# Expert gate and up projections in groups of 1024 columns, over two PSUM banks each

## The reference, cut to what matters

```python
def swiglu(h, w_gate, w_up, w_down):
    return (jax.nn.silu(h @ w_gate) * (h @ w_up)) @ w_down
...
for e in range(N_EXPERTS):
    y = y + combine[..., e:e + 1] * swiglu(h, w_gate[e], w_up[e], w_down[e])
```

## Time and profile before

| | |
|---|---|
| median of 3 runs | 1862.31 us (1860.47 to 1862.36) |
| the profiled execution | 1858.9 us, of which the span of its instructions is 1857.2 us |
| PE busy | 1701.4 us, 92% of the span |
| DVE busy | 1293.8 us, 70% |
| ACT busy | 1052.4 us, 57% |
| moved by DMA | 491.7 MB, 265 GB/s over the span |
| span of the items' loop | 825.2 to 1835.6 us |
| from one item's `YE` to the next one's | 126.1 to 126.2 us, twice about 124.4 us |

### The profile page before, as it was taken

One profiled execution on the slowest core, in us unless ns is written; L12 is line 12 of the kernel. 1 busy time (PEld: TensorE's weight loads), 2 busy tenths in 40 slices (PEclk: granted clock), 3 DMA queues, 4 the chain that ended last, 5 costly groups with the idle time before them and its releaser, 6 DMA issues.

```text
span 1857.2 us, 24273 instructions
## 1 busy us (share of the span) xinstructions
PE 1701.4 (92%) x9295; PEld 1464.4 (79%) x9295; DVE 1293.8 (70%) x1092; ACT 1052.4 (57%) x915; POOL 72.8 (4%) x94
## 2 busy tenths in 40 slices
PE   4986989998999887939999999999999999999995
PEld 4964989998999777928878878778788787787884
DVE  3796255545954256348878878888788788787885
ACT  3534244434342156237777777677777776777772
POOL 2014000000000100010000000000000000000001
PEclk9998799999987799969999999999999999999997
DMA  6525059656566223639999999999999999999992
GB/s 237 179 68 161 21 176 336 224 171 197 167 197 226 85 71 104 229 126 349 380 318 396 359 329 387 341 356 374 320 390 364 320 393 356 349 378 329 377 369 82
DMA packets 236653, 491.70 MB, mean 265 GB/s; under 512 B 8665, under 2 KB 66137, under 8 KB 236328
## 3 DMA queue, kind: packets, MB, share of 16 engines
q1 hardware_dynamic: 227088, 456.60, 68.6%
q0 software_dynamic: 9504, 34.24, 5.5%
HBM read 463.87 MB, written 27.42 MB: 265 GB/s over the span
## 4 chain that ended last, share of the span: by engine, by line
issue 57%; PE 31%; DVE 8%; ACT 2%; DMA 1%; POOL 1%; POOLq 0%; SPq 0%; ACTq 0%; DVEq 0%
PE bank L613 7%; PE bank L614 7%; PE bank L615 7%; PE bank L893 2%; DVE WL L1395 2%; PE bank L831 1%; DVE even_CA L1454 1%; ACT WH L1109 1%; PE bank L728 1%; DVE RS L1469 1%; DMA R<-in_param 1%; DVE RS L1642 1%; PE bank L882 1%; POOL moe_rows_in L593 0%; ACT L1301 0%
## 5 line engine op out<-in xcount | busy, mean ns | idle before, releaser
L1740 DVE TENSOR_TENSOR WL<-moe_MORE,WH 128x2048 fp32r<-128x2048 f32 x192 | 439.3, 2291 | 120.7 <-ACT WH L1323 120.7
L1323 ACT ACTIVATE WH<-moe_MORE 128x2048 fp32r<-128x2048 f32 x192 | 368.4, 1923 | 181.7 <-PE bank L615 181.6
L1740 DVE TENSOR_TENSOR WL<-ring,WH 128x2048 fp32r<-128x2048 f32 x144 | 329.0, 2289 | 49.9 <-ACT WH L1323 48.9
L613 PE MATMUL bank<-WH,moe_XEH 128*128 128x512 f32 x896 | 360.2, 402 | 3.7 <-DVE moe_XEL L1746 2.3
L615 PE MATMUL bank<-WH,moe_XEL 128*128 128x512 f32 x896 | 354.9, 396 | 0.0
L614 PE MATMUL bank<-WL,moe_XEH 128*128 128x512 f32 x896 | 354.9, 396 | 0.0
L1323 ACT ACTIVATE WH<-ring 128x2048 fp32r<-128x2048 f32 x144 | 275.9, 1918 | 91.2 <-PE bank L615 91.2
L613 PE MATMUL bank<-HH,WH 128*128 128x264 f32 x960 | 283.3, 295 | 19.3 <-DVE HL L1413 18.2
L1395 DVE TENSOR_TENSOR WL<-ring,WH 128x2048 fp32r<-128x2048 f32 x80 | 181.0, 2263 | 152.1 <-ACT WH L1109 151.9
L614 PE MATMUL bank<-HL,WH 128*128 128x264 f32 x960 | 279.7, 291 | 0.0
L615 PE MATMUL bank<-HH,WL 128*128 128x264 f32 x960 | 279.3, 291 | 0.0
(11 more groups left out here) (307 smaller groups left out, 1869.6 us busy)
## 6 DMA issues: line engine op xcount, KB each, us to landing
moe_MORE<-in_moe_w_gate SPq DMA_DIRECT2D x72, 1024.0 KB, 6.7
moe_MORE<-in_moe_w_up SPq DMA_DIRECT2D x72, 1024.0 KB, 6.7
ring<-in_moe_w_down SPq DMA_DIRECT2D x64, 1024.0 KB, 7.3
moe_MORE<-in_moe_w_down SPq DMA_DIRECT2D x48, 1024.0 KB, 5.2
ring<-in_moe_w_gate SPq DMA_DIRECT2D x40, 1024.0 KB, 5.5
ring<-in_moe_w_up SPq DMA_DIRECT2D x40, 1024.0 KB, 7.0
ring<-in_w_in_odd SPq DMA_DIRECT2D x24, 1024.0 KB, 5.2
ring<-in_ffn_w_gate SPq DMA_DIRECT2D x11, 1024.0 KB, 7.6
```

The source lines that it names most:

```text
L613: mm(out, lh, rh, start=start, stop=False)
L1323: func(WH[:, q % WRING, :], chunk(q), ACT.Copy).then_inc(s_hi, 1)
L1740: V.tensor_tensor(WL[:, q % WRING, :], chunk(q), full(WH[:, q % WRING, :]), ALU.subtract)\
```

## The change

Steps are joined in `GROUPS`: (0, 1), (2, 3), (4, 5) and (6,). For a group of two, gate is computed for 1024 columns in four chunks of two k-tiles each, then up in four chunks, then the down projections of the two steps of the group before, two chunks each. A matmul is still 512 columns wide; in a chunk, three matmuls go to one bank and three to the other (gate 2 and 3, up 6 and 7). The number of chunks (42), matmuls (504) and bytes is as before. HBM is read in runs of 4 KB by gate and up as well.

The turned hidden rows have bank 1 for all steps. A group turns its two steps one after the other: PE does `turn_hidden(before[0])` behind the gate chunks, and `turn_hidden(before[1])` behind the up chunk i = 1, with a new wait on `s_atl`, since DVE must have read bank 1 first. ACT and DVE do `turned` on the up chunks i = 1 and 2 (in the last group, which has two up chunks, on i = 0 and 1), `turned(6)` on down (4, 1).

The next item's rows are turned in two rounds of four transposes through bank 0, behind the up chunks of groups 1 and 2. ACT copies each round as float32 to a new tile `XTB`. Near the item's end, on down (5, 0), ACT makes `XEH` of `XTB` in one instruction of 1024 columns, and DVE then `XEL` in one. The load of these rows is issued at chunk 14 instead of 24, and `YE` is written back at chunk 10 instead of 12. One semaphore of the first stage is merged with another.

```diff
 FW = 512
 MSTEPS = FE // FW
+GROUPS = [(0, 1), (2, 3), (4, 5), (6,)]
 MHID = 4 * MSTEPS
...
         XG = region("moe", "XG", D)
+        XTB = region("moe", "XTB", DK, P)
         XEH = region("moe", "XEH", DK, P, dt=F32R)
         XEL = region("moe", "XEL", DK, P, dt=F32R)
...
-        for f in range(MSTEPS):
-            ORDER += [("gate", f, 0), ("gate", f, 1), ("up", f, 0), ("up", f, 1)]
-            ORDER += [("down", f - 1, 0), ("down", f - 1, 1)] if f >= 1 else []
+        for g, steps_of in enumerate(GROUPS):
+            ORDER += [(kind, g, i) for kind in ("gate", "up") for i in range(2 * len(steps_of))]
+            ORDER += [("down", f, i) for f in (GROUPS[g - 1] if g >= 1 else ()) for i in range(2)]
         ORDER += [("down", MSTEPS - 1, 0), ("down", MSTEPS - 1, 1)]
         PLACE = {key: c for c, key in enumerate(ORDER)}
         X_FIRST = MRING + WRING - 1
-        X_NEXT = 24
-        Y_BACK = 12
+        X_NEXT = 14
+        Y_BACK = 10
 
         def taps(g):
 
...
+                for c, (kind, g, i) in enumerate(ORDER):
                     if kind == "down":
-                        r0 = f * FW + half * FW // 2
...
                     else:
                         w = m_gate if kind == "gate" else m_up
-                        src = w[0, bass.ds(e, 1), half * 512:half * 512 + 512, f * FW:(f + 1) * FW]\
+                        wide = FW * len(GROUPS[g])
+                        rows = P * CW // wide
+                        src = w[0, bass.ds(e, 1), i * rows:(i + 1) * rows, 2 * g * FW:2 * g * FW + wide]\
                             .rearrange("o (k p) n -> p (o k) n", p=P)
                     q = C_MOE + c
                     if isinstance(it, int) and c < MRING:
...
 
             load_expert(0, 0)
...
@@ -1019,38 +1024,50 @@
             pe.wait_ge(s_items, 1)
             n_items = pe.value_load(EII[0:1, TI_N:TI_N + 1], min_val=E, max_val=MAXI)
 
-            def turn_in(it):
-
-                pe.wait_ge(s_xl, it * 16 + 16)
-                for k in range(DK):
-                    last = turn(PB[k // 4][:, (k % 4) * P:(k % 4 + 1) * P], XG[:, k * P:(k + 1) * P], ident)
+            def turn_in(it, half):
+
+                if half == 0:
+                    pe.wait_ge(s_xl, it * 16 + 16)
+                if half == 1 or not isinstance(it, int):
+                    pe.wait_ge(s_xtb, it * 2 + half)
+                for k in range(4):
+                    at = (4 * half + k) * P
+                    last = turn(PB[0][:, k * P:(k + 1) * P], XG[:, at:at + P], ident)
                 last.then_inc(s_xtp, 1)
 
             pe.wait_ge(s_hx, 2 * NT)
-            turn_in(0)
+            turn_in(0, 0)
+            turn_in(0, 1)
             with pe.Fori(0, n_items) as it:
-                def hidden(kind, f):
...
-                        if f == 0:
-                            pe.wait_ge(s_xeh, it * 2 + 2)
-                            pe.wait_ge(s_xel, it * 2 + 2)
+                def hidden(kind, g, i):
+
+                    banks = (PB[2], PB[3]) if kind == "gate" else (PB[6], PB[7])
+                    wide = len(GROUPS[g])
+                    nk = CW // (FW * wide)
+                    if i == 0 and kind == "gate":
+                        if g == 0:
+                            pe.wait_ge(s_xel, it + 1)
                         else:
-                            pe.wait_ge(s_si, it * MSTEPS + f)
-                    for half in range(2):
-                        q = C_MOE + PLACE[(kind, f, half)]
-                        pe.wait_ge(s_lo, it * MCH + (q + 1))
-                        wh, wl = (x.rearrange("p (k n) -> p k n", n=FW) for x in parts(q))
-                        for kk in range(4):
-                            k = 4 * half + kk
-                            last = mm3(PB[2 if kind == "gate" else 3][:, :], XEH[:, k, :], XEL[:, k, :],
-                                       wh[:, kk, :], wl[:, kk, :], k == 0, k == DK - 1)
-                        last.then_inc(s_mm, 1)
+                            pe.wait_ge(s_si, it * MSTEPS + 2 * g)
+                    if i == 0 and kind == "up" and g >= 1:
+                        pe.wait_ge(s_ac, it * MSTEPS + 2 * g)
+                    q = C_MOE + PLACE[(kind, g, i)]
+                    pe.wait_ge(s_lo, it * MCH + (q + 1))
...
+                    for kk in range(nk):
+                        k = nk * i + kk
+                        for b in range(wide):
+                            cols = slice(b * FW, (b + 1) * FW)
+                            last = mm3(banks[b][:, :], XEH[:, k, :], XEL[:, k, :],
+                                       wh[:, kk, cols], wl[:, kk, cols], k == 0, k == DK - 1)
+                    last.then_inc(s_mm, 1)
 
                 def turn_hidden(f):
                     pe.wait_ge(s_ac, it * MSTEPS + f + 1)
+                    if f >= 1:
+                        pe.wait_ge(s_atl, it * MSTEPS + f)
                     for j in range(4):
...
-                    hidden("gate", f)
-                    if f >= 1:
-                        turn_hidden(f - 1)
-                    hidden("up", f)
-                    if f == 4:
-                        turn_in(it + 1)
-                    if f >= 1:
-                        project_down(f - 1, 0)
-                        if f == MSTEPS - 1:
-                            turn_hidden(f)
-                        project_down(f - 1, 1)
+                for g, fs in enumerate(GROUPS):
+                    before = GROUPS[g - 1] if g >= 1 else ()
+                    for i in range(2 * len(fs)):
+                        hidden("gate", g, i)
+                    if before:
+                        turn_hidden(before[0])
+                    for i in range(2 * len(fs)):
+                        hidden("up", g, i)
+                        if before and i == 1:
+                            turn_hidden(before[1])
+                    if 1 <= g <= 2:
+                        turn_in(it + 1, g - 1)
+                    if before:
+                        project_down(before[0], 0)
+                        project_down(before[0], 1)
+                        if g == len(GROUPS) - 1:
+                            turn_hidden(MSTEPS - 1)
+                        project_down(before[1], 0)
+                        project_down(before[1], 1)
                 project_down(MSTEPS - 1, 0)
                 project_down(MSTEPS - 1, 1)
...
-                act.wait_ge(s_xtp, it + 1)
-                for i in range(2):
-                    func(XEH[:, 4 * i:4 * i + 4, :], PB[i][:, :].rearrange("p (k n) -> p k n", n=P), ACT.Copy)\
-                        .then_inc(s_xeh, 1)
-
-            copy_in(0)
+            def copy_in(it, half):
+                act.wait_ge(s_xtp, it * 2 + half + 1)
+                if not isinstance(it, int):
+                    act.wait_ge(s_xel, it)
+                func(XTB[:, 4 * half:4 * half + 4, :], PB[0][:, :].rearrange("p (k n) -> p k n", n=P), ACT.Copy)\
+                    .then_inc(s_xtb, 1)
+
+            def high_in(it):
+                act.wait_ge(s_xtb, it * 2 + 2)
+                func(XEH[:, :, :], XTB[:, :, :], ACT.Copy).then_inc(s_xeh, 1)
+
+            copy_in(0, 0)
+            copy_in(0, 1)
+            high_in(0)
             with act.Fori(0, n_items) as it:
                 def turned(f):
                     act.wait_ge(s_at, it * MSTEPS + f + 1)
                     if f >= 2:
                         act.wait_ge(s_dn, it * MDN + 2 * (f - 1))
-                    func(ATH[:, f % 2, :], PB[6][:, :], ACT.Copy).then_inc(s_ate, 1)
-
-                for c, (kind, f, half) in enumerate(ORDER):
+                    func(ATH[:, f % 2, :], PB[1][:, :], ACT.Copy).then_inc(s_ate, 1)
+
+                def silu(f):
+                    g = f // 2
+                    act.wait_ge(s_mm, it * MHID + 8 * g + 2 * len(GROUPS[g]))
+                    if f >= 2:
+                        act.wait_ge(s_ac, it * MSTEPS + f - 1)
+                    func(SI[:, f % 2, :], PB[2 + f % 2][:, :], ACT.Silu).then_inc(s_si, 1)
+
+                for c, (kind, g, i) in enumerate(ORDER):
                     if c + WRING < MCH:
                         high_moe(it, c + WRING)
-                    if kind == "gate" and half == 1:
-                        act.wait_ge(s_mm, it * MHID + 4 * f + 2)
-                        if f >= 2:
-                            act.wait_ge(s_ac, it * MSTEPS + f - 1)
-                        func(SI[:, f % 2, :], PB[2][:, :], ACT.Silu).then_inc(s_si, 1)
-                        if f >= 1:
-                            turned(f - 1)
-                    if (kind, f, half) == ("up", MSTEPS - 1, 1):
+                    if kind == "gate" and i == 2 * len(GROUPS[g]) - 1:
+                        silu(GROUPS[g][0])
+                    if kind == "up" and g < 3:
+                        if i == 0:
+                            silu(GROUPS[g][1])
+                        if g >= 1 and i in (1, 2):
+                            turned(GROUPS[g - 1][i - 1])
```

(104 more changed lines are left out.)

5 lines of the change are left out of this document (2 added, 3 removed).

## The result

The changed kernel takes 1976.44 us, the median of 4 runs (1975.21 to 1978.88), against 1862.34 us (1860.47 to 1863.71). The ratio is 1.0617, with a 95% interval of 1.0602 to 1.0632: it is slower by 114 us, where 107 were forecast.

The account below looks back on a forecast made before the run. PE sets the pace, busy 123.5 of an item's 126.1 us. Per item 126.1 - 2.6 - 1.5 + 10.4 + 2.4 + 3 x 1.5 = 139.3; 8 x 13.2 + 1.4 = 107 us more, 1969 us, range 1944 to 1992.

Parts of the forecast that it names:

- The new stops: PE waits for ATL behind chunks 13 and 25, 5.2 us each, and behind chunk 35, 2.4 us, in every item.
- the rival in which it stays up: PE's clock stays at full through the new stops: 8.7 us more an item, kernel at 1933 us; chance 0.05.
- the rival of more stops: Spare times of 0.2 to 1.0 us fail: at 3 us an item, 1993 us or more; chance 0.06.
- the prediction's first rival: ATL(0) is there before PE ends chunk 13, so the new stops go: kernel at 1831 us; chance 0.03.
- The item's end: Ahead of chunk 40 the old stop of 2.6 us goes, with 1.0 us to spare.
- the banks and the runs of 4 KB: In gate and up chunks, turns of banks cost nothing; longer runs can only help a queue that runs ahead.
- The slow clock: PE at half clock behind each of an item's three new stops, taken as 1.5 us each.
- The low bound: Part of the slow stretch falls into the stop: 0.8 us for each stop of 5.0 us, nothing in the last group.
- The sum: An item grows by 13.2 us to 139.3; eight items and the start give 107 us more.
- The first item's start: Between the transposes and the first matmul, 3.6 us instead of 2.27: 1.4 us more, once, bounds 0 and 3.

Follow-up runs that it names:

- experiment 5: The changed kernel with hidden rows turned through two banks, turn_hidden not waiting for s_atl, turn_in one chunk later, and turned left late: 1850.18 us.
- experiment 7: The changed kernel with turned of a group's first step on the same chunk, but ahead of WH and WL instead of behind them: 1881.71 us.
- Experiment 1: The changed kernel with turned of a group's first step moved earlier on ACT and DVE, to the last gate chunk, in all three groups: 1830.62 us.
- Experiment 3: The kernel before the change with only turned of step 6 moved earlier on ACT and DVE, and low_in on DVE with it: 1828.91 us.
- experiment 4: The changed kernel with turned moved to the last gate chunk in groups 2 and 3 only, leaving group 1's stop of 5.0 us: 1893.02 us.
- experiment 2: The changed kernel with turned moved to the last gate chunk in groups 1 and 2 only, leaving the last group's stop: 1860.42 us.
- experiment 6: The changed kernel with turned moved to the last gate chunk except in group 2, whose stop of 5.0 us is left: 1891.81 us.

## Why the prediction was right, point by point

**The new stops: right in place, number and size.** The forecast had 5.43 us from the last matmul to PE's restart and 5.0 of them idle, twice an item, and 2.2 idle in the last group. The trace has 5.41, 5.02 and 2.24, in all eight items. The clock went to half behind all 24, so the rival in which it stays up falls, and there are no stops beyond the 24 and the short one that was there before, so the rival of more stops falls too. Experiments 5 and 7 show the chain's parts: without the shared bank nothing waits at chunk 13, and without `WH` and `WL` of chunk 16 the stop shrinks to 2.24 us. Experiment 1 shows that nothing else stood there; with 1830.6 us it ends where the prediction's first rival, `ATL` in time, put such a kernel, 1831.

**The item's end: right.** The wait for `ATL` ahead of chunk 40 is gone, in the changed kernel and in experiment 1. In the item shown, `ATL` of step 6 ends at 1105.05, and chunk 40 starts 1.0 us later, as counted:

```profile
1104.37 0.68 DVE L1798 TENSOR_TENSOR moe_ATL<-bank,moe_ATH 128x512 fp32r<-128x512 f32 x1
...
1106.03 0.39 PE L618 MATMUL bank<-WH,moe_ATH 128*128 128x512 f32 x1
```

Experiment 3 shows that this gain, 34.6 us against the kernel before measured beside it, needed `turned(6)` moved on ACT and DVE, `low_in` moved with it, and none of the rest.

**No cost and no gain from the banks and the runs of 4 KB: right.** Experiments 1 and 3 have the same item to 0.1 us. In experiment 1, with three matmuls to one bank and three to the other, fifteen starts take 999.50 - 996.00 = 3.50 us, the same 0.233 us a matmul:

```profile
996.00 0.39 PE L620 MATMUL bank<-WH,moe_XEL 128*128 128x512 f32 x1
...
999.50 0.39 PE L620 MATMUL bank<-WH,moe_XEL 128*128 128x512 f32 x1
```

Both experiments move 370 GB/s over a whole item. The Trainium skill ("DMA: Bandwidth & Descriptors", its table of specifications) gives about 358 GB/s as one core's half of a stack's 716 GB/s. Here one core ran, and that figure did not hold an item up.

**The slow clock: the term that was too small.** I took 1.5 us for each of the three stops, 4.5 an item, from a stop of 2.42 us. Against experiment 1 it is 5.2 us (18.0 less the delays of 12.8). Counted by starts in the item shown, the loss is 2.1 us behind the first stop, with its 4.5 us of half clock, and 1.6 behind each of the two others. So the part that I sized wrong is the first stop of 5.0 us; the second, just as long, cost what I took. That the two differ I had not foreseen, and what sets it stays open: alone, the same stop costs 1.8 to 2.6 us from one item to the next (experiment 4). All of it lay inside the bounds that I gave for a stop of 5.0 us, 0.8 and 2.6 us. The low bound was for a slow stretch that begins in the stop; it did begin there in the first stop, and the loss was still 2.1 us.

**The sum.** The forecast had 107.0 us for the span, and the spans differ by 117.3. Of the 10.3 us between them the items have 5.2, which is the missing slow clock, some 0.7 us in each of the eight: from the first matmul of the loop to the last copy of `YE` it was 1011.1 us and is 1121.9, 110.8 more against 105.6. The first item's start has 0.5, with 6.1 us from the first transpose to the first matmul instead of 4.2, 1.9 more against 1.4:

```profile
824.73 1.08 PE L1035 MATMUL bank<-C,moe_XG 128*128 128x128 f32 x4 [22.93 <-DMA moe_XG<-moe_rows_in]
825.85 0.60 ACT L1367 ACTIVATE moe_XTB<-bank 128x512 f32<-128x512 f32 x1 [16.95 <-PE bank L1035]
...
830.81 0.79 PE L618 MATMUL bank<-WH,moe_XEH 128*128 128x512 f32 x1 [3.19 <-DVE moe_XEL L1786]
```

The last 0.9 lie behind the loop, and 3.8 ahead of it, where the transposes start at 824.73 and not at 820.97. In the profiles of the eight experiments they start between 822.1 and 824.7. The kernels made from the changed one start at 823.7 in the mean of seven, 822.6 to 824.7, and those with the old first stage at 822.0 in the mean of three, 821.0 to 823.0. The means differ by 1.7 us and the ranges overlap, so about half of the 3.8 us, or more, is scatter from one execution to another; whether the merged semaphore or another part of the change has a share in it was not tested and stays open. Half of the 10.3 us thus lies outside the items. The medians, of four runs each, differ by 114.1 us.

## What to carry to other kernels

Where an engine walks a list and does small pieces "behind" a large copy that waits for a slot, each piece inherits that wait: ask for each new wait of the bound engine not only which instruction ends it, but what stands ahead of that instruction in its own queue, and what that waits for. When steps are joined into groups, the pieces between them have to move by as many chunks as their reader did. A late piece becomes a stop where its reader comes soon, or where the next piece needs the same buffer (experiment 5). Before a regrouping is judged by what it was paired with, do the small reordering alone: here it gave the whole gain.

## What the runs showed of the hardware that I had not expected

An idle time of PE of 2.2 us was followed by a half clock in some items and not in others of the same kernel, with the same work in each (124.3 and 125.9 us in experiment 2, 126.7 and 129.9 in experiment 7). It came behind 6 of 8 such stops in experiment 2, 9 of 16 in experiment 7, and all 8 in the last group of the changed kernel. An idle time of 1.8 us was never followed by it, in the 8 items of experiment 5, and one of 5.0 us always, 16 times in the changed kernel and 8 in each of experiments 4 and 6. The loss of matmul time was 1.6 us behind a short one. Behind a stop of 5.0 us it was 2.1 and 1.6 us for the two of an item in the changed kernel, and 1.8 to 2.6 us where there was one such stop an item (experiment 4, from the second item on). And a single core moved 370 GB/s for whole items, weights and the items' rows together, with runs of 2 KB as with runs of 4 KB.
